# One VectorE comparison for all eight one-hot rows of a lot in the scatter stage, ScalarE copying only

## What is computed

```python
cand_i = si[:, :, 0, :, None] * PEER_NKEYS + si[:, :, 1, None, :]      # expert number = i * 128 + j
best_s, best_p = lax.top_k(cand_s.reshape(...), PEER_TOPK)
idx = jnp.take_along_axis(cand_i.reshape(...), best_p, axis=-1)
gate = jax.nn.softmax(best_s, axis=-1)
act = jnp.einsum('td,thkd->thk', xb, u_tab[ib])
wgt = jax.nn.gelu(act) * gb
y = jnp.einsum('thk,thkd->td', wgt, v_tab[ib])
```

## Time and profile before

| | us |
|---|---|
| Median of 3 runs | 3481.14 |
| Lowest and highest | 3479.04, 3497.25 |
| Profiled execution, its time | 3481.03 |
| Its span in the profile | 3479.0 |
| TensorE busy | 3333.5 (96%) |
| VectorE busy | 2443.6 (70%) |
| ScalarE busy | 1766.0 (51%) |
| GpSimd busy | 522.9 (15%) |

### The profile page before, as it was taken

The page is one execution under the profiler, slowest core; times in us unless marked ns, Lnnn a source line. Parts: engine busy times, 40 slices in busy tenths (PEclk is TensorE's granted clock), DMA queues, the critical chain, the costliest instruction groups (busy, mean ns, idle before and its releaser), DMA issues. The chain is left out here.

```text
span 3479.0 us, 65019 instructions
## 1 busy us (share of the span) xinstructions
PE 3333.5 (96%) x20516; PEld 2887.0 (83%) x20516; DVE 2443.6 (70%) x4853; ACT 1766.0 (51%) x3349; POOL 522.9 (15%) x428
## 2 busy tenths in 40 slices
PE   7999999999989998999899999999999889999999
PEld 5767776778769998889778999998789778999998
DVE  6657776767566775569877777776659877777776
ACT  4443343333356655646754545444656754454544
POOL 0000000000000001558720000000648730000000
PEclk9989999999999998999999999999999999999999
DMA  5125434435215554335045555555335135555554
GB/s 206 40 76 177 164 130 133 139 121 164 73 61 175 165 175 153 110 124 173 18 139 187 187 187 187 187 187 178 122 111 169 48 109 188 187 186 187 187 187 157
DMA packets 139223, 508.82 MB, mean 146 GB/s; under 512 B 15968, under 2 KB 16352, under 8 KB 138208
## 3 DMA queue, kind: packets, MB, share of 16 engines
q1 hardware_dynamic: 138384, 504.56, 45.0%
q10 hardware_dynamic: 720, 2.71, 0.2%
HBM read 506.16 MB, written 1.05 MB: 146 GB/s over the span
## 5 line engine op out<-in xcount | busy, mean ns | idle before, releaser
L286 ACT ACTIVATE split<-ring 128x512 fp32r<-128x512 f32 (+1 forms) x1700 | 1061.4, 628 | 1393.1 <-PE ps L217 1328.5
L293 DVE TENSOR_TENSOR split<-ring,split 128x512 fp32r<-128x512 f32 (+1 forms) x1404 | 956.9, 686 | 638.5 <-ACT split L286 617.1
L217 PE MATMUL ps<-h2T,split 128*128 128x256 f32 x7776 | 982.2, 284 | 7.6 <-DVE gates L2006 4.7
L217 PEld LDWEIGHTS ps<-h2T,split 128*128 128x128 f32 x7776 | 964.9, 192 | 29.5 <-DVE gates L2006 5.1
L217 PE MATMUL ps<-split,chunk 128*128 128x512 f32 x3072 | 735.3, 391 | 2.8 <-DVE chunk L2535 2.8
L293 POOL TENSOR_TENSOR split<-ring,split 128x512 fp32r<-128x512 f32 x296 | 389.4, 1332 | 2239.9 <-ACT split L286 2233.4
L217 PEld LDWEIGHTS ps<-split,chunk 128*128 128x128 f32 x3072 | 563.8, 188 | 113.9 <-DVE chunk L2535 4.0
L217 PE MATMUL ps<-hT,split 128*128 128x512 f32 (+1 forms) x3504 | 635.9, 341 | 9.7 <-DVE split L293 5.8
L217 PEld LDWEIGHTS ps<-hT,split 128*128 128x128 f32 x3504 | 537.3, 188 | 106.2 <-DVE hT L529 13.1
L2391 PE MATMUL ps<-ring 128*128 128x128 f32 x1024 | 146.8, 288 | 42.6 <-POOL ring L2379 27.1
L217 PE MATMUL ps<-act_chunk,split 128*128 128x512 f32 (+1 forms) x1056 | 186.1, 337 | 0.0
(11 more groups left out here) (348 smaller groups left out, 3133.4 us busy)
## 6 DMA issues: line engine op xcount, KB each, us to landing
ring<-peer_uv SPq DMA_DIRECT2D x456, 512.0 KB, 3.5
ring<-w_up SPq DMA_DIRECT2D x88, 512.0 KB, 3.8
ring<-w_choose SPq DMA_DIRECT2D x88, 512.0 KB, 3.6
ring<-w_mixing SPq DMA_DIRECT2D x68, 512.0 KB, 3.5
ring<-w_merge SPq DMA_DIRECT2D x64, 512.0 KB, 4.2
ring<-w_down SPq DMA_DIRECT2D x44, 512.0 KB, 3.6
mix_row_ring<-w_mod SPq DMA_DIRECT2D x40, 512.0 KB, 3.6
ffn_row_ring<-w_mod SPq DMA_DIRECT2D x40, 512.0 KB, 4.0
```

The costliest lines, as they stand in the source:

```text
L217: ins = nc.tensor.matmul(out, lhsT(a), rhs(b), start=first and n == 0, stop=last and n == len(PASSES) - 1)
L286: self.nc.scalar.activation(self.split[:, s % SPLIT, 0, cols], self.ring[:, s, cols], ACT.Copy).then_inc(self.high_ready, 1)
L293: (ops or self.nc.vector).tensor_tensor(self.split[:, s % SPLIT, 1, cols], self.ring[:, s, cols], self.split[:, s % SPLIT, 0, cols].bitcas ...
```

## The change

All eight one-hot rows of a lot, four of hot_i and four of hot_j, lie one behind the other in one buffer hot, as [lot of the turn, row, 128]. The keys are kept in one table slot_key, laid out as [lot, i or j, token of the lot], so that the eight keys of a lot are neighbours. VectorE writes the eight rows with one comparison of 128 x 1024, which signals one_hot once. GpSimd waits for that signal and multiplies the first four rows by the gates. ScalarE writes no one-hot row any more, and its program is a plain loop over keep. TensorE has one wait less. VectorE keeps lag 2.

```diff
-            for n, x in enumerate((k.slot_i, k.slot_j, k.slot_gate)):
-                nc.vector.tensor_copy(x[:, :], k.ps[:, RAW + n, 0:SEQ]).then_inc(slots_ready, 1)
+            for n, x in enumerate((k.slot_key[:, :, 0, :], k.slot_key[:, :, 1, :], k.slot_gate.rearrange("p (l t) -> p l t", t=LOT))):
+                nc.vector.tensor_copy(x, k.ps[:, RAW + n, 0:SEQ].rearrange("p (l t) -> p l t", t=LOT)).then_inc(slots_ready, 1)
...
-    on_act = 1
+    many = 2 * lot
...
-    iota = iota_psum.unsqueeze(1).broadcast_to([P, lot, NK])
+    iota = iota_psum.unsqueeze(1).broadcast_to([P, many, NK])
+    slot_keys = k.slot_key.rearrange("p l s t -> p (l s t)")
...
             def one_hots(i, n):
                 dve.wait_ge(spread, i * lots + n + 1)
-                for hot, slot, first in ((k.hot_i, k.slot_i, 0), (k.hot_j, k.slot_j, on_act)):
-                    many = lot - first
-                    keys = slot[:, bass.ds(token(i, n) + first, many)].unsqueeze(2).broadcast_to([P, many, NK])
-                    nc.vector.tensor_tensor(hot[:, n * lot + first:(n + 1) * lot, :], iota[:, 0:many, :], keys,
-                                            ALU.is_equal).then_inc(one_hot, 1)
+                keys = slot_keys[:, bass.ds(token(i, n) * 2, many)].unsqueeze(2).broadcast_to([P, many, NK])
+                nc.vector.tensor_tensor(k.hot[:, n, 0:many, :], iota, keys, ALU.is_equal).then_inc(one_hot, 1)
...
-                    pool.wait_ge(one_hot, (i * lots + n) * 2 + 1)
-                    hot = k.hot_i[:, n * lot:(n + 1) * lot, :]
+                    pool.wait_ge(one_hot, i * lots + n + 1)
+                    hot = k.hot[:, n, 0:lot, :]
...
-                    pe.wait_ge(one_hot, (i * lots + n) * 2 + 2)
-                    pe.wait_ge(act_hot, i * lots + n + 1)
+                    pe.wait_ge(one_hot, i * lots + n + 1)
...
-            def one_hots(i, n):
-                act.wait_ge(spread, i * lots + n + 1)
-                hot = k.hot_j[:, n * lot, :]
-                nc.scalar.activation(hot, k.const("iota"), ACT.Abs, scale=-1.0,
-                                     bias=k.slot_j[:, bass.ds(token(i, n), 1)]).then_inc(distance, 1)
-                act.wait_ge(distance, i * lots + n + 1)
-                nc.scalar.activation(hot, hot, ACT.Relu, scale=-1.0, bias=1.0).then_inc(act_hot, 1)
...
-            lagged(act, one_hots, keep, 1)
+            with act.Fori(0, turns_all) as i:
+                for n in range(lots):
+                    keep(i, n)
...
-    k.slot_i, k.slot_j, k.slot_gate = (sb(scope, f"slot_{n}", SEQ) for n in ("i", "j", "gate"))
+    k.slot_key, k.slot_gate = sb(scope, "slot_key", SEQ // LOT, 2, LOT), sb(scope, "slot_gate", SEQ)
...
-    k.hot_i, k.hot_j = hot(16, NK), hot(16, NK)
+    k.hot = Carver(k.ring.rearrange("p s m -> p (s m)"))(4, 2 * LOT, NK)
```

More of the change, by code:

```diff
@@ L73 @@
 EARLY = 28
-RAW, SPLIT = 4, 2
+RAW, SPLIT, LOT = 4, 2, 4
 SUMS_LATE = 3
@@ L2321, in _ @@
             dve.wait_ge(turned, 1)
-            for n, x in enumerate((k.slot_i, k.slot_j, k.slot_gate)):
-                nc.vector.tensor_copy(x[:, :], k.ps[:, RAW + n, 0:SEQ]).then_inc(slots_ready, 1)
+            for n, x in enumerate((k.slot_key[:, :, 0, :], k.slot_key[:, :, 1, :], k.slot_gate.rearrange("p (l t) -> p l t", t=LOT))):
+                nc.vector.tensor_copy(x, k.ps[:, RAW + n, 0:SEQ].rearrange("p (l t) -> p l t", t=LOT)).then_inc(slots_ready, 1)
 def scatter_stage(k):
-    nc, lot, lots, late = k.nc, 4, 4, NK - EARLY
+    nc, lot, lots, late = k.nc, LOT, 4, NK - EARLY
     turns_all = SEQ // (lots * lot)
-    on_act = 1
+    many = 2 * lot
     iota_psum = k.ps[:, 7, 0:NK]
-    iota = iota_psum.unsqueeze(1).broadcast_to([P, lot, NK])
+    iota = iota_psum.unsqueeze(1).broadcast_to([P, many, NK])
+    slot_keys = k.slot_key.rearrange("p l s t -> p (l s t)")
     token = lambda i, n: (i * lots + n) * lot
@@ L2348, in lagged @@
             keep(turns_all - 1, n)
-    with stage(nc, "one_hot", "gated", "spread", "copied", "weighted", "distance", "act_hot") as (
-            block, one_hot, gated, spread, copied, weighted, distance, act_hot):
+    with stage(nc, "one_hot", "gated", "spread", "copied", "weighted") as (
+            block, one_hot, gated, spread, copied, weighted):
         @block.vector
@@ L2386, in _ @@
                     pe.wait_ge(weighted, i * lots + n + 1)
-                    pe.wait_ge(one_hot, (i * lots + n) * 2 + 2)
-                    pe.wait_ge(act_hot, i * lots + n + 1)
+                    pe.wait_ge(one_hot, i * lots + n + 1)
                     pe.wait_ge(gated, i * lots + n + 1)
                     for u in range(lot):
-                        last = nc.tensor.matmul(k.ps[:, n, u * NK:(u + 1) * NK], k.hot_i[:, n * lot + u, :],
-                                                k.hot_j[:, n * lot + u, :], start=True, stop=True)
+                        last = nc.tensor.matmul(k.ps[:, n, u * NK:(u + 1) * NK], k.hot[:, n, u, :],
+                                                k.hot[:, n, lot + u, :], start=True, stop=True)
                     last.then_inc(spread, 1)
@@ L2584, in second_block @@
     k.weight = k.chunk
-    k.slot_i, k.slot_j, k.slot_gate = (sb(scope, f"slot_{n}", SEQ) for n in ("i", "j", "gate"))
+    k.slot_key, k.slot_gate = sb(scope, "slot_key", SEQ // LOT, 2, LOT), sb(scope, "slot_gate", SEQ)
     k.gelu, k.gated = sb(scope, "gelu", 2, SEQ), sb(scope, "gated", SEQ)
-    hot = Carver(k.ring.rearrange("p s m -> p (s m)"))
-    k.hot_i, k.hot_j = hot(16, NK), hot(16, NK)
+    k.hot = Carver(k.ring.rearrange("p s m -> p (s m)"))(4, 2 * LOT, NK)
     gates = sb(scope, "gates", SEQ * NK)
```

## The result

The changed kernel is slower: 1.0078 times the time of before (95% interval 1.0063 to 1.0093), which is 27 us. The means of the six runs of each, 3513.0 and 3485.6 us, differ by 27 us, their medians, 3515.2 and 3480.1 us, by 35 us. The profiled execution took 3504.06 us with a span of 3502.3 us, 23.3 us above the span of before.

What follows compares the result with a forecast made beforehand. A chain across engines from comparison to weighing, once per three lots, was taken as the bound. Its lengthening costs 10.8 us in each of two scatter stages: 3481.0 + 21.6 = 3502.6 us, 0.62% slower, range 3493 to 3511.

Steps and rivals of the forecast that it cites:

- What bounds the kernel: Scatter stages: a 3.97 us chain plus 0.27 gap, once per three lots, allows 1.413 us a lot; VectorE's work 1.32.
- (a): VectorE: two comparisons become one of 1024 elements, 1225 ns; it holds VectorE 1.14 us start to start instead of 1.07.
- (b): GpSimd's gate product waits for all eight rows, starting 1.405 us after the comparison's start, not 0.87: 0.535 us more chain.
- (c): ScalarE loses two activations a lot, 45 us a stage, from spare time: worth nothing, at best 0.1 us of the chain.
- (d): Key table copies before the stage: may each cost twice their 0.42 us, still hidden in VectorE's 2.65 us idle time.
- (e): VectorE's queue: weigh_early's wait for the copied gates grows; VectorE idle some 0.5 us or more before most weighings.
- The sum: Scatter stages: chain with gap 4.775 us over three lots, 1.592 us a lot; 10.8 us more per stage, 21.6 for two.
- VectorE's interference: Scatter lots: VectorE's own work adds 0.016 us to the period before; not added after, its 1.39 being well below 1.592.
- such a longer start: Start of each scatter stage: if only this lengthens because TensorE's clock falls, it is 1 us.
- VectorE's work as the bound: Rival, scatter stages: VectorE's work bounds and copies come in time; period 1.39, 5 us gained, 3476 us; chance 0.06.
- A link shortened by an idle ScalarE: Rival, chain: idle ScalarE or fewer waits shorten a link by up to 0.1 us; 4.3 us less, 3498.3; chance 0.14.
- the third: Rival, scatter stages: TensorE's clock falls, matmuls take 1.94 us instead of 1.13; 35 us more, 3537 us; chance 0.04.

Runs made afterwards that it cites:

- the kernel before with lags 3 and 2: Kernel before with VectorE's lag raised from 2 to 3 and ScalarE's from 1 to 2: 0.9925 times the time of before.
- before with the late product: Kernel before with only GpSimd's wait moved, so its gate product waits for both comparisons of the lot: 1.0057 times the time of before.

## Why the prediction was right

The direction, the mechanism and the size held: 21.6 us were forecast, 24.8 us are in the two stages, 23 to 27 us in the time. By the ratio the changed kernel stands at 3507 us, within the range of 3493 to 3511 us, but the median of its six executions, 3515 us, lies above it. The range had only a few microseconds for differences between executions, and these are some 20 us wide, so whether a measured time falls into it is partly luck.

- What bounds the kernel: right. The chain of a lot returns every third lot, shown by lag 3 with nothing else changed, which took 9.0 and 10.4 us off the stages of the kernel before. That VectorE's own work came nearly to the same was wrong in part: VectorE's own work is 1.25 us a lot (the two stages of the kernel before with lags 3 and 2 run at 1.26 and 1.25), not 1.32, for there the loop's turn adds nothing.
- (a) The comparison of 1024 elements: 1225 ns forecast, 1223 measured. Start to start 1.14 forecast, 1.13 with lag 3 (1699.81 to 1700.94).
- (b) GpSimd's start: 1.405 forecast, 1.40 measured, and a wait moved by itself costs 10 us a stage. This was the decisive step.
- (c) ScalarE's relief worth nothing: right, shown by the run that kept ScalarE busy (1.607 us a lot against 1.609).
- (d) The copies of the key table: 0.42 us each as before, and the same idle time of 2.65 us follows them.
- (e) The wait before the weighing grew, but its figure was wrong: I expected 0.5 us and more before most weighings. By my own sum the two bounds lie 1.59 - 1.39 = 0.20 us a lot apart, and VectorE is idle 90.00 - 79.74 = 10.3 us in the middle window above, 0.18 us a lot. It comes in pieces, such as 0.38 at 1693.29, and much of it is under what the view lists.
- The sum is 1.6 us a stage too small (10.8 against 12.4). Of the terms, 59 lots at 1.609 instead of 1.592 make 1.0 us of it. I had set VectorE's interference at nothing, and it is still there: some weighings wait for the comparison ahead of them, and the mean of comparison to weighing over the stage after its first lots is 4.54 us, not 4.505; the gap after it is 0.28, not 0.27. The first five comparisons make 0.4 us: they take 7.40 us instead of 6.32 before, and I had put 0.64 for it. There the clock shows. The matmuls of the first three lots took 2.05, 1.91 and 1.91 us, where before they took 2.04, 1.53 and 1.13 (the prediction reckoned the first of these as 1.94); the granted clock of the first 8.5 us was 0.60 against 0.80. The prediction named such a longer start at 1 us, but did not add it. Whether the change lengthened the stretch of lower clock stays open: all four profiled stages of the changed kernel and both of before with the late product have 0.60, but the changed kernel with ScalarE busy had 0.61 in one stage and 0.80 in the other, and as two comparisons, with the product as early as before, it had 1.00 and 0.60. The last weighing ends 4.68 us after the last comparison's start instead of 4.03, 0.1 us more than I put.
- The rivals: VectorE's work as the bound fell (it would have been a gain of 5 us). A link shortened by an idle ScalarE fell: from product to copy it is 2.47 us after and 2.46 to 2.48 before. The clock in the stage is 1.00 after its beginning, so the third fell but for the first three lots.

## What to carry to other kernels

Before merging instructions, ask who waits for the first part of the result: the signal of a merged instruction comes at its end, and here 0.53 us more on a chain across four engines went with 12 us a stage, 10 of them shown by the wait alone, while the merged instruction itself held VectorE only 0.07 us longer than the two. Overlapping instructions are to be compared from start to start, since their durations count the overlap twice. Where a loop makes something for lot n and then waits for what comes back of lot n - lag, divide the length of the round trip by lag + 1 and compare it with the work of each engine; if it is the longer, the lag is the thing to change (lag 3 and 2 instead of 2 and 1 gave 0.7% here), and an edit of the work moves nothing or makes it worse. Each engine in the circle has its own order, and the next one comes to light when the first is mended.

## What was unexpected of the hardware

At the turn of the loop the gap from a weighing's start to the next comparison is 0.38 and 0.51 us in the earlier trace rows and up to 0.55 us in the changed kernel, where inside a turn it is 0.18 to 0.23. The traces show a simple relation: the comparison after the turn starts 0.62 to 0.69 us after the end of the copy for which the weighing waited, or 0.18 us after the weighing's start, whichever is later. Where the copy ended 0.12 to 0.14 us before the weighing the gap is 0.50 to 0.55, at 0.24 it is 0.38, at 0.37 (before with lag 3, second stage) 0.25, and at 0.7 (all turns of the changed kernel with lag 3) 0.18, so that the turn costs nothing. Read as the instructions of the turn being handled once the wait is over, while the engine works, this fits, but it was not tested by itself. And the executions of one kernel differ by 2.5 us for each 0.001 of the mean granted clock, so that a change of 20 us is as large as their spread; comparing at the same clock (23.4 us, with a standard error of 0.8) was sharper than comparing medians.
